# Expert results written to memory by token and choice, and added back in the last expert

## The reference, cut to what matters

```python
probs = jax.nn.softmax(jnp.einsum('btd,de->bte', h, w_router), axis=-1)
top_v, top_i = lax.top_k(probs, TOP_K)                     # TOP_K = 2 of 8 experts
top_v = top_v / jnp.sum(top_v, -1, keepdims=True)
combine = jnp.sum(jax.nn.one_hot(top_i, N_EXPERTS) * top_v[..., None], axis=-2)
y = jnp.zeros_like(h)
for e in range(N_EXPERTS):
    y = y + combine[..., e:e + 1] * swiglu(h, e_gate[e], e_up[e], e_down[e])
...
x = layer_norm(ALPHA * x + gt2 * f_out, ln2_w[l], ln2_b[l])   # f_out is y here
```

## Time and profile before

| what | value |
|---|---|
| device time, median of 3 runs | 1512.11 us (1511.02 to 1513.95) |
| device time of the profiled execution | 1512.35 us |
| its span, first to last instruction | 1510.6 us |
| TensorE busy | 1461.3 us (97%) |
| VectorE busy | 1169.6 us (77%) |
| ScalarE busy | 908.7 us (60%) |
| GpSimd busy | 46.2 us (3%) |
| moved by DMA | 416.22 MB |
| mean granted TensorE clock | 0.989 of full speed |

### The profile page before, as it was taken

One profiled execution on the slowest core, in us unless ns is written; L12 is line 12 of the kernel. 1 busy time (PEld: TensorE's weight loads), 2 busy tenths in 40 slices (PEclk: granted clock), 3 DMA queues, 4 the chain that ended last, 5 costly groups with the idle time before them and its releaser, 6 DMA issues.

```text
span 1510.6 us, 24730 instructions
## 1 busy us (share of the span) xinstructions
PE 1461.3 (97%) x9772; PEld 1275.5 (84%) x9772; DVE 1169.6 (77%) x1240; ACT 908.7 (60%) x867; POOL 46.2 (3%) x84
## 2 busy tenths in 40 slices
PE   5999999999999999999999999999999999999995
PEld 4899989999998998867888888888878888888884
DVE  2455796556668667859889889898898888988988
ACT  2645565323334665646777676676766766777774
POOL 2000100000000100010000000000000000000000
PEclk9999999999999999999999999999999999999998
DMA  9989467355445732547999999999999999999995
GB/s 331 356 306 328 144 197 267 131 167 168 140 137 188 241 126 65 177 140 250 347 351 351 339 358 337 342 359 330 352 342 338 359 335 339 359 342 365 350 372 193
DMA packets 217752, 416.22 MB, mean 276 GB/s; under 512 B 7920, under 2 KB 79770, under 8 KB 217639
## 3 DMA queue, kind: packets, MB, share of 16 engines
q1 hardware_dynamic: 214086, 402.31, 76.4%
q0 software_dynamic: 3552, 12.33, 2.7%
HBM read 407.80 MB, written 6.82 MB: 274 GB/s over the span
## 4 chain that ended last, share of the span: by engine, by line
PE 56%; DVE 3%; issue 1%; ACT 1%; DMA 0%; DVEq 0%; ACTq 0%
PE bank L702 16%; PE bank L704 16%; PE bank L703 16%; PE bank L1227 1%; PE bank L1265 1%; PE bank L705 1%; PE bank L706 1%; PE bank L707 1%; DVE w_lo L1813 1%; PE bank L1320 1%; PE bank L1321 1%; PE bank L843 0%; PE bank L1176 0%; DMA raw_ring<-in_e_gate_dram 0%; PE bank L1060 0%
## 5 line engine op out<-in xcount | busy, mean ns | idle before, releaser
L1813 DVE TENSOR_TENSOR w_lo<-raw_ring,w_hi 128x2048 fp32r<-128x2048 f32 x265 | 606.5, 2291 | 95.8 <-ACT w_hi L1505 95.0
L1505 ACT ACTIVATE w_hi<-raw_ring 128x2048 fp32r<-128x2048 f32 x266 | 510.5, 1919 | 229.6 <-PE bank L704 224.7
L702 PE MATMUL bank<-w_hi,xg_hi 128*128 128x512 f32 (+1 forms) x768 | 293.2, 382 | 0.9 <-DVE w_lo L1813 0.7
L704 PE MATMUL bank<-w_hi,xg_lo 128*128 128x512 f32 (+1 forms) x768 | 288.9, 376 | 0.0
L703 PE MATMUL bank<-w_lo,xg_hi 128*128 128x512 f32 (+1 forms) x768 | 288.8, 376 | 0.0
L705 PE MATMUL bank<-act_hi,w_hi 128*128 128x320 f32 x720 | 227.3, 316 | 6.3 <-DVE act_lo L1868 5.8
L706 PE MATMUL bank<-act_lo,w_hi 128*128 128x320 f32 x720 | 223.1, 310 | 0.0
L707 PE MATMUL bank<-act_hi,w_lo 128*128 128x320 f32 x720 | 223.0, 310 | 0.0
L1804 DVE TENSOR_TENSOR w_lo<-raw_ring,w_hi 128x2048 fp32r<-128x2048 f32 x65 | 148.6, 2287 | 68.6 <-ACT w_hi L1419 68.4
L704 PEld LDWEIGHTS bank<-w_hi,xg_lo 128*128 128x128 f32 x768 | 144.3, 188 | 29.3
L702 PEld LDWEIGHTS bank<-w_hi,xg_hi 128*128 128x128 f32 x768 | 144.4, 188 | 26.7 <-DVE w_lo L1813 1.1
(11 more groups left out here) (366 smaller groups left out, 1866.1 us busy)
## 6 DMA issues: line engine op xcount, KB each, us to landing
raw_ring<-in_e_gate_dram SPq DMA_DIRECT2D x90, 1024.0 KB, 5.2
raw_ring<-in_e_up_dram SPq DMA_DIRECT2D x90, 1024.0 KB, 5.5
raw_ring<-in_e_down_dram SPq DMA_DIRECT2D x88, 1024.0 KB, 5.2
raw_ring<-in_w_ada_dram SPq DMA_DIRECT2D x32, 1024.0 KB, 7.1
raw_ring<-in_w_in_dram SPq DMA_DIRECT2D x24, 1024.0 KB, 7.1
raw_ring<-in_w_ff_gate_dram SPq DMA_DIRECT2D x11, 1024.0 KB, 5.5
raw_ring<-in_w_ff_up_dram SPq DMA_DIRECT2D x11, 1024.0 KB, 5.4
raw_ring<-in_w_ff_down_dram SPq DMA_DIRECT2D x11, 1024.0 KB, 4.9
```

Of the source, the lines that this page charges most:

```text
L702: pe.matmul(out, xh, wh, start=start, stop=False)
L704: return pe.matmul(out, xl, wh, start=False, stop=stop)
L1505: act.activation(w_hi[:, (NSPLIT + i) % SPL, :], raw[:, s, :], ACT.Copy).then_inc(hi_ready.sem, 1)
L1813: dve.tensor_tensor(w_lo[:, r, :], raw[:, s, :], w_hi[:, r, :].bitcast(F32), ALU.subtract).then_inc(lo_ready.sem, 1)
```

## The change: what it does

For experts 0 to 6 the product with GT goes away. `token_map` multiplies G only with the weights and a new third group of `spread`: for each token and expert a row number, 128 + token + 320 x rank, where rank (0 or 1) says whether the expert is the token's first or second choice. VectorE makes from it the weight and the row number of each slot (`slot_rows`); an empty slot gets one of the rows 0 to 127, which nobody reads. `weighted` now makes one float32 tile: ScalarE columns 0 to 511, VectorE 512 to 1023, in two buffers in turn. GpSimd writes the 128 rows with an indirect DMA to `y_rows` in memory (768 x 1024), whose rows 128 to 767 it has set to zero at the start of the stage with five writes of 0.5 MB. In the last expert GpSimd reads `y_rows` back in six pieces (three token tiles, two choices), each when TensorE has used a certain chunk (PACE). VectorE adds the two choices of a tile (`sum_choices`), TensorE transposes the sum in five steps through bank 0 (`turn_sums`), and VectorE adds it, times the gate, to `xT` (`sums_added`). `flush_prompt` and `flush_samples` go. The LayerNorm rows are loaded behind the last piece. The eight scatter steps of the last expert are as before.

```diff
@@ gpsimd @@
+            with pool.Fori(0, rounds) as rd:
...
+                pool.memset(y_buf[0], 0.0).then_inc(ticked.sem, 1)
+                tick_at(2)
+                for i in range(Y_ZERO):
+                    pool.dma_start(y_rows[P * (i + 1):P * (i + 2), :], y_buf[0]).then_inc(y_moved.sem, 16)
+                for e in range(NE - 1):
+                    pool.wait_ge(wsl_ready.sem, wsl_ready.at(rd, e))
+                    pool.wait_ge(yw_hi.sem, yw_hi.at(rd, e))
+                    pool.wait_ge(yw_lo.sem, yw_lo.at(rd, e))
+                    pool.wait_ge(y_moved.sem, rd * Y_TURN + 16 * (Y_ZERO + e))
+                    tick_at(3 + e)
+                    pool.indirect_dma_start(y_rows, bass.IndirectOffsetOnAxis(ids[:, e:e + 1], 0), y_buf[e % 2],
+                                            None).then_inc(y_moved.sem, 16)
+                pool.wait_ge(*y_free(rd, NE - 1))
+                for n, (kind, b, part) in enumerate(PACE):
+                    t, j = divmod(n, 2)
+                    pool.wait_ge(w_used.sem, w_used.at(rd, MOE_AT[NE - 1, kind, b, part]))
...
+                    pool.dma_start(dst, y_rows[t0:t0 + VTILES[t][2], :]).then_inc(y_back[t].sem, 16)
@@ before the engines @@
+        Z_STEPS = [(0, 0, 4), (0, 4, 4), (1, 0, 4), (1, 4, 4), (2, 0, KD)]
+        PACE = [("up", 1, 1), ("gate", 2, 0), ("up", 2, 0), ("down", 1, 0), ("gate", 3, 0), ("up", 3, 0)]
@@ tensor @@
                 for t, t0, n in VTILES:
-                    last = pe.matmul(bank[0][:, MW * t + P - n:MW * (t + 1)], G[0:n, t, e, :], spread[0:n, t, P - n:MW],
-                                     start=True, stop=True)
...
+                        last = pe.matmul(bank[0][:, 0:MW - P], G[0:n, t, e, :], spread[0:n, t, P:MW],
+                                         start=(t == 0), stop=(t == NT - 1))
...
+            def turn_sums(rd, s):
+                t, m0, nm = Z_STEPS[s]
+                n = VTILES[t][2]
+                if s:
+                    pe.wait_ge(sc_read.sem, sc_read.at(rd, s - 1))
...
+                if m0 == 0:
+                    pe.wait_ge(flushed.sem, flushed.at(rd, 1 + t))
+                if n < P:
+                    pe.transpose(bank[0][:, 0:P], ident[:], ident[:])
+                for m in range(m0, m0 + nm):
+                    z = back[t // 2][0:n, t % 2, m * P:(m + 1) * P]
+                    last = pe.transpose(bank[0][:, (m - m0) * n:(m - m0 + 1) * n], z, ident[0:n, 0:n])
+                last.then_inc(sc_mm.sem, 1)
...
                         if parts[b] == 2:
                             gate_up(rd, e, "gate", b, 1)
-                        if b < 3 and e:
-                            scatter(rd, e - 1, 6 * (b - 1))
+                        if b == 4 and last_of:
+                            turn_sums(rd, 0)
                         gate_up(rd, e, "up", b, 0)
-                        if b < 3 and e:
-                            scatter(rd, e - 1, 6 * (b - 1) + 1)
+                        if b == 4 and last_of:
+                            turn_sums(rd, 1)
                         if parts[b] == 2:
                             gate_up(rd, e, "up", b, 1)
...
+                        if b == 4 and last_of:
+                            turn_sums(rd, 2)
+                        if b == NEB - 1 and last_of:
+                            turn_sums(rd, 3)
...
                 down(rd, NE - 1, NEB - 2, 0)
                 turn(rd, NE - 1, NEB - 1)
+                turn_sums(rd, 4)
                 down(rd, NE - 1, NEB - 2, 1)
@@ vector @@
+            def sum_choices(rd, t):
+                dve.wait_ge(y_back[t].sem, rd * 32 + 32)
...
+                dve.tensor_tensor(z, z, other, ALU.add).then_inc(flushed.sem, 1)
...
+            def sums_added(rd, s):
...
+                dve.wait_ge(sc_mm.sem, sc_mm.at(rd, s))
...
+                if t < 2:
+                    for m in range(m0, m0 + nm):
+                        last = dve.scalar_tensor_tensor(xT[:, m, t0:t0 + n], bank[0][:, (m - m0) * n:(m - m0 + 1) * n],
+                                                        modT[:, 5 * KD + m, 0:1], xT[:, m, t0:t0 + n], ALU.mult, ALU.add)
+                    last.then_inc(sc_read.sem, 1)
+                    return
...
                         if parts[b] == 2:
                             used(rd, e, "gate", b, 1)
+                        if b == 4 and last_of:
+                            sums_added(rd, 0)
                         if parts[b] == 1:
                             gated(rd, e, b)
                         used(rd, e, "up", b, 0)
-                        if e == NE - 1 and b in (3, 4):
-                            flush_prompt(rd, range(4 * (b - 3), 4 * (b - 2)))
+                        if b == 4 and last_of:
+                            sums_added(rd, 1)
...
                             gated(rd, e, b)
                             used(rd, e, "up", b, 1)
+                        if b == 4 and last_of:
+                            sum_choices(rd, 1)
+                            sums_added(rd, 2)
+                            sum_choices(rd, 2)
+                        if b == NEB - 1 and last_of:
+                            sums_added(rd, 3)
...
                             used(rd, e, "down", b - 1, 0)
+                            if b == 3 and last_of:
+                                sum_choices(rd, 0)
                             used(rd, e, "down", b - 1, 1)
                 used(rd, NE - 1, "down", NEB - 2, 0)
                 turned(rd, NE - 1, NEB - 1)
+                sums_added(rd, 4)
```

More of the change, by code:

```diff
@@ L272, in hybrid_trunk @@
         xg_hi, xg_lo = ([a[i] for a in (xg0, xg1)] for i in range(2))
+        y_rows = nc.dram_tensor("y_rows", [P + 2 * T, D], F32, kind="Internal").ap()
+        y_buf = [y_two[:, i, :] for i in range(2)]
+        back = [choice[:, 0:2, :], choice[:, 2:4, :],
+                accT[:].rearrange("p k t -> p (k t)")[:, 0:2 * D].rearrange("p (j d) -> p j d", d=D)]
+        gated_s = accT[:].rearrange("p k t -> p (k t)")[:, 2 * D:2 * D + KD * TS].rearrange("p (k s) -> p k s", s=TS)
+        Y_ZERO = 2 * T // P
+        Y_TURN = 16 * (Y_ZERO + NE - 1)
+        PACE = [("up", 1, 1), ("gate", 2, 0), ("up", 2, 0), ("down", 1, 0), ("gate", 3, 0), ("up", 3, 0)]
         banks = ctx.enter_context(nc.psum_tensor("bank", [P, 8, 512], F32))
@@ L687, in hybrid_trunk @@
         TOP_K = 2
[L688 removed]
+        MW = P + 3 * NE
         NROWS = 7 * DEPTH + 1
@@ L1304, in token_map @@
-                last.then_inc(GT_mm.sem, 1)
-            def scatter(rd, e, m):
-                b = bank[scatter_bank(e, m)]
-                if m == 0:
-                    pe.wait_ge(GT_read.sem, GT_read.at(rd, e))
-                    pe.wait_ge(wsl_ready.sem, wsl_ready.at(rd, e))
-                    if e < NE - 2:
-                        pe.wait_ge(xg_lo_ready.sem, xg_lo_ready.at(rd, NF * (e // 2 + 1) + 2 * (e % 2) + 1))
-                elif e < NE - 1 or m >= 5:
-                    pe.wait_ge(sc_read.sem, sc_read.at(rd, KD * e + m - (1 if e < NE - 1 else 5)))
-                if m == 1 and e == NE - 1:
+                    if e == NE - 1:
+                        last = pe.matmul(bank[0][:, MW * t + P - n:MW * (t + 1)], G[0:n, t, e, :], spread[0:n, t, P - n:MW],
+                                         start=True, stop=True)
+                    else:
+                        last = pe.matmul(bank[0][:, 0:MW - P], G[0:n, t, e, :], spread[0:n, t, P:MW],
+                                         start=(t == 0), stop=(t == NT - 1))
@@ L1317, in scatter @@
+            def scatter(rd, m):
+                b = bank[scatter_bank(m)]
+                if m == 0:
+                    pe.wait_ge(GT_read.sem, GT_read.at(rd))
+                elif m >= 5:
+                    pe.wait_ge(sc_read.sem, sc_read.at(rd, m))
+                if m == 1:
                     pe.wait_ge(ea_ready.sem, ea_ready.at(rd, NE * NEB - 1))
                 if m % 4 == 0:
-                    pe.wait_ge(yw_lo.sem, yw_lo.at(rd, 2 * e + m // 4))
+                    pe.wait_ge(yw_lo.sem, yw_lo.at(rd, NE - 1 + m // 4))
@@ L1347, in experts @@
                             turn(rd, e, 0)
-                        if b == 2 and e:
-                            scatter(rd, e - 1, 5)
+                        last_of = e == NE - 1
                         if b in (3, 4) and more:
```

175 lines of the change are left out of this document (96 added, 79 removed).

## The result

The changed kernel took 1520.83 us (median of 5 runs, 1519.3 to 1524.3), the kernel before, on the same chip, 1513.95 (5 runs, 1511.02 to 1514.82). The ratio is 1.0042, 95% interval [1.0025, 1.0059]: slower by 6.4 us (3.8 to 8.9). The forecast was 1511.0, its range ended at 1518. The spans of the profiled executions differ by 8.1 us, 1510.6 to 1518.7.

The account below looks back on a forecast made before the run. TensorE was taken to bound the expert stage. The terms -19.4 + 2.9 + 9.1 + 3.5 + 2.5 + 0.2 = -1.2 us gave 1511 us from a median of 1512.11, with an eight-in-ten range of 1503.5 to 1518.

Parts of the forecast that it names:

- Removal: TensorE, experts 0 to 6: 56 scatter steps save 16.8 us, a scatter's wait 0.9, smaller token maps 1.7; sum -19.4 us.
- Transposes: TensorE, last expert: the five steps' transposes add 0.5 us for each of the first four, 0.9 for the last; +2.9 us.
- Waits of the steps: Last expert: TensorE waits for VectorE at steps 1, 2 and 4, 2.2, 5.7 and 1.9 us; 9.8 us in sum.
- Clock: Behind the three step waits TensorE's clock falls: long wait charged 1.7 us, two short ones 0.9 each; +3.5 us.
- DMA traffic: Last expert: 4.19 MB of extra traffic, 11.2 us at 375 GB/s, mostly absorbed; +2.5 us, ends 0 and 9.3.
- The catch-up of 3.8 us: Last expert: loads need a little less than 2.8 us each, gaining 0.19 us a load over 20 chunks, 3.8 us.
- The slack of the landing: Last expert: a landing of 6.9 us costs nothing, median 5.1; with another 1.2 us, 3.0 us of traffic is absorbed.
- Rival B: Last expert, up(1,1) to gate(4,1): bound by its loads, the ring running dry; price 9.3 instead of 2.5, 1517.7 us; chance 0.15.
- Small things and zero fill: One short VectorE operation adds +0.2 us; the 2.6 MB of zeros at the start get nothing, ends 0 and 2 us.
- A: Last expert: the short waits don't lower the clock and the ring absorbs the traffic; 1506.6 us, chance 0.24.
- D: Last expert: the steps don't make TensorE wait, and the clock loss goes with the waits; 1497.6 us, chance 0.08.
- C: Every write after an expert reaches TensorE (7 x 1.4 us) and the zeros delay the first chunks (2); 1522.7 us, chance 0.06.

Follow-up runs that it names:

- experiment 3: The changed kernel without the six read-backs, the sums of choices and the five steps, seven experts' results left out of the output: 1496.07 us, ratio 0.9886.
- experiment 9: The kernel before with one unused one-column tensor, which moves the stationary operands of the expert matmuls to multiples of 64 bytes: 1506.77 us, ratio 0.9944.
- experiment 1: The changed kernel with VectorE's adding one position earlier and TensorE's steps 1, 2 and 4 one or two chunks later: 1506.81 us, ratio 0.9953.
- experiment 6: The changed kernel with its six read-backs cut from 1024 to 16 columns of a row: 1516.01 us, ratio 1.0001.
- experiment 8: The changed kernel with reordered steps, later LayerNorm rows, and the zero writes moved behind chunk up(1,0) of the first expert: 1509.54 us, ratio 0.9966.

## Why the prediction was wrong

**Removal** (forecast -19.4, measured -18.1 between the maps, -18.0 in experiment 3). The interval of the earlier trace rows fell by 2.40 us, of which 0.09 are the map; that is 0.29 a step and 16.2 us for 56. But the falls weren't alike: 2.28 us between the maps of experts 2 and 3, which use xg1, and 2.66 and 2.68 where both experts use xg0. Matmuls of 512 columns followed each other there in 0.2332 and 0.2342 us before, and in 0.2333 everywhere after (means of the traces). By this estimate the steps are worth 15.3 us (0.27 each) and about 1 us of the 18.1 is layout, as in experiment 9. The scatter's wait went as forecast. The token map was mis-sized: 0.51 became 0.42 us, 0.6 in all instead of 1.7, though its columns fell from 144 to 24.

**Transposes** (+2.9): 2.7 us in experiment 1. Right.

**Waits of the steps** (9.8 us of waits): 9.58, and place, releaser and size of each came out. Reading the two engines' orders side by side and adding the durations of the earlier trace rows was enough. Steps 0 and 3 don't wait.

**Clock** (+3.5, range to 5.3). T to the first scatter grew by 16.4: 9.6 of new waits, less the old 0.7, and 2.9 of transposes leave 4.6 us. The stretches behind the three waits of the changed kernel show it directly (columns as in the earlier trace rows):

```profile
1459.00:1464.00 5.00, 4.69 (x16) 3.76 (x16) 3.49 (x6) 0.12 (x1) 0.00 (x0) 0.66 1.02 362
1470.00:1475.00 5.00, 5.00 (x18) 4.10 (x18) 2.25 (x5) 0.08 (x1) 0.00 (x0) 0.66 0.50 196
1490.00:1495.00 5.00, 5.00 (x19) 3.92 (x18) 3.68 (x3) 0.00 (x1) 0.00 (x0) 0.66 0.50 189
```

Each is 5 us at 0.66, the same 1.7 us as in the earlier trace rows, and 5.1 in all. So the mechanism was right and the two short waits were under-sized: they cost in full and not at half. The term is within its range, at its upper end.

**DMA traffic** (+2.5, range to 9.3). This step failed. Measured are +8.3 us from the last token map to T, and 8.4 by experiment 6, which takes the bytes away. 5.6 us of it are waits for low halves, and 1.6 the lower clock of the chunk behind the longest (1449.34 to 1453.78 is 4.44 us instead of 2.81). The remaining 1.1 go with the five waits themselves: around each the starts of the matmuls lie some 0.2 to 0.3 us further apart than the bracket and the usual spacing say. Two of the terms that were to absorb the 11.2 us were far smaller than I had them:
- *The catch-up of 3.8 us.* I had read from landings that fell by 0.19 us a load that a load needs less than a chunk's 2.81 us. At the 381 GB/s that the engines reached at share 1.04, a weight load of 1.05 MB takes 2.75 us of them: 0.06 a chunk, 1.2 over 20. A falling landing time tells how the ring fills, not how fast the engines are. Share 1.00 stood in the earlier trace rows.
- *The slack of the landing.* I set 6.9 us against a median of 5.1. The change itself had used some of it up: with experts shorter by 2.4 us and the writes beside them, the median of the landings is 5.7 us over 1100 to 1200 against 5.2 before, and over the whole kernel 5.9 to 6.1 against 5.2 to 5.5.

With 11.0 us for the 4.19 MB at 381 GB/s, 1.2 of catch-up, and a slack of 6.9 - 5.9 + 1.2 = 2.2, the same sum gives 11.0 - 2.6 - 1.2 - 2.2 = 5.0 us of waits, and 5.6 were measured. This sum is made afterwards, with the rate and the landings of the changed kernel, and no run tests its two terms apart; what experiment 6 shows is that the bytes make the waits. To this the clock had to be added, which I had charged for the steps only. Rival B, "the last expert becomes bound by its loads", named the mechanism, its place (up to gate(4,1)) and nearly its price (9.3), and I gave it 0.15. The landings went past the 8 us from which it was to decide.

What spoke against the limit of 358 GB/s was right: the engines reached 381. The Trainium skill has this too, in "Perfetto Trace Analysis", section "Roofline": one core alone can go over its share of 358 GB/s, up to about 120% of it. The trace agrees: 381 is 106%. But the error lay in treating the distance between 355 and 375 as the question. Even at 381 the term was 8.3 us. (Two sums of the prediction are slightly off: its own terms give 9.2 for the 9.3 and 8.5 for the 8.7. Nothing hangs on it.)

**Small things and zero fill** (0, range to 2): 0.1 to 0.7 for the zero fill (experiment 8), and 0.85 us of the difference of the spans is no effect of the change.

The sum with the measured terms: -18.1 + 16.4 + 8.3 + 1.5 = +8.1, the difference of the spans. The forecast had -1.2; of the 9.3 us between them 5.8 are the traffic, 1.5 the start, 1.3 the removal and 0.7 the waits with their clock. The terms aren't independent: with the bytes taken away (6) the wait of step 1 is longer, and only 6.4 us are gained at the end of the stage. Without the 5.8 us of the traffic the change would have come out inside the forecast's range.

Rivals: A fell on both counts, D by the three waits. C is refuted in its first part, as experts 1 to 6 show no wait.

## What to carry to other kernels

A change that makes a loop shorter takes from the slack of everything that was hidden in it: reckon the landing times of the loads for the new period before extra bytes are set against them, and never count both a slack and a catch-up unless the DMA share is clearly under 1. Where an engine's order is written by hand, put short work that another engine waits for ahead of the long operation, not behind; here that was worth 15 us. And when an edit that can't touch a loop makes it faster, compare the addresses of its operands and run a control before the edit is judged. The same holds for the edit under test itself: one unused column in both kernels took the difference between them from 6.6 to 0.3 us of stage time, because it helped one more than the other.

## What the runs showed of the hardware

- *Zeros among loads.* 2.6 MB written while the ring is being filled for the first expert cost 5.3 us more up to the first token map than when they are issued some 30 us earlier; seven writes of 0.52 MB in running experts cost nothing that TensorE's waits show.
